# Gate and up products of 20 of 22 FFN tiles per layer: one level of Strassen's seven block products in the place of eight

## The reference

```
r = r + rms_norm(y, g_mix_post[i])
h = rms_norm(r, g_ffn_pre[i])
y = (silu(h @ w_gate[i]) * (h @ w_up[i])) @ w_down[i]      # D_FF = 2816
r = r + rms_norm(y, g_ffn_post[i])
# ... then a gated per-layer input embedding
```

## Time and profile before

| | |
|---|---|
| median of 3 runs | 3164.13 us (3160.27 to 3171.47) |
| profiled execution, span from first to last instruction | 3166.1 us |
| mean granted TensorE clock | 0.975 |
| TensorE busy | 3004.7 us, 95% |
| DVE busy | 2039.4 us, 64% |
| ACT busy | 982.9 us, 31% |
| POOL busy | 1426.3 us, 45% |
| FFN of layer 0, loop over tiles | about 759 to 1418 us of the span |
| FFN of layer 1, loop over tiles | about 2285 to 2944 us of the span |

### The profile page before, as it was taken

How to read it: one execution, slowest core, us unless ns; L and a number is a source line. 1 busy time by engine, 2 the same in 40 slices (tenths; PEclk the granted TensorE clock), 3 DMA queues, 4 the chain that set the end, 5 groups by cost and what they waited for, 6 DMA issues and landing times.

```text
span 3166.1 us, 54358 instructions
## 1 busy us (share of the span) xinstructions
PE 3004.7 (95%) x18978; PEld 2901.6 (92%) x18978; DVE 2039.4 (64%) x3685; ACT 982.9 (31%) x2197; POOL 1426.3 (45%) x933
## 2 busy tenths in 40 slices
PE   7999999999999999998988999999899999999887
PEld 7889999988999999998887988889899999999887
DVE  4657888465655655567574589965655655665675
ACT  4234777341000000004442177743300000000252
POOL 4233555554433433345554455545533433343564
PEclk9999999999999999999989999999899999999988
DMA  3497444311111111111102566522111111111111
GB/s 112 166 325 243 132 127 126 108 34 41 48 45 46 40 52 40 46 48 60 41 21 103 191 152 154 136 74 74 40 41 46 46 46 42 44 53 40 55 47 55
DMA packets 163131, 264.63 MB, mean 84 GB/s; under 512 B 95056, under 2 KB 108896, under 8 KB 162640
## 3 DMA queue, kind: packets, MB, share of 16 engines
q1 hardware_dynamic: 163024, 263.21, 26.7%
HBM read 197.74 MB, written 65.42 MB: 83 GB/s over the span
## 4 chain that ended last, share of the span: by engine, by line
PE 65%; issue 13%; POOL 11%; DVE 6%; ACT 2%; DMA 1%; POOLq 0%; SPq 0%; DVEq 0%; ACTq 0%
PE ps L1329 31%; PE ps L1039 11%; PE ps L1040 11%; PE ps L1041 11%; POOL probs L936 8%; DVE sublayer_out L2063 1%; PE ps L1060 1%; POOL pre_sums L896 1%; PE ps L1074 1%; DVE act_lo L2078 1%; POOL weight_hi L860 1%; DVE post_sums L2039 1%; DVE pre_sums L2039 1%; DVE stage_lo L2162 1%; DMA kA_lo<-stage_lo 1%
## 5 line engine op out<-in xcount | busy, mean ns | idle before, releaser
L860 POOL TENSOR_TENSOR weight_hi<-weight_raw,ones 128x1024 fp32r<-128x1024 f32 x179 | 353.0, 1972 | 1170.7 <-PE ps L1041 611.3
L2308 DVE TENSOR_TENSOR sublayer_out<-ps,sublayer_out 128x352 f32<-128x352 f32 x1008 | 527.7, 524 | 515.4 <-PE ps L1041 506.7
L1329 PE MATMUL ps<-act_hi,weight_hi 128*128 128x352 f32 x2112 | 686.4, 325 | 10.1 <-ACT ffn_act L1740 4.8
L1329 PE MATMUL ps<-act_hi,weight_lo 128*128 128x352 f32 x2112 | 683.8, 324 | 0.0
L1329 PE MATMUL ps<-act_lo,weight_hi 128*128 128x352 f32 x2112 | 683.8, 324 | 0.0
L1039 PE MATMUL ps<-act_hi,weight_hi 128*128 128x352 f32 (+2 forms) x1392 | 472.5, 339 | 32.3 <-DVE weight_lo L2107 10.8
L874 POOL TENSOR_TENSOR weight_lo<-weight_raw,weight_hi 128x1024 fp32r<-128x1024 f32 x193 | 477.3, 2473 | 54.4 <-ACT weight_hi L1730 28.3
L1040 PE MATMUL ps<-act_lo,weight_hi 128*128 128x352 f32 (+2 forms) x1392 | 459.6, 330 | 0.0
L1041 PE MATMUL ps<-act_hi,weight_lo 128*128 128x352 f32 (+2 forms) x1392 | 459.3, 330 | 0.0
L936 POOL TENSOR_TENSOR probs<-probs,row_inv 128x1024 f32<-128x1024 f32 (+8 forms) x288 | 312.1, 1093 | 291.7 <-DVE row_inv L2240 291.4
L1329 PEld LDWEIGHTS ps<-act_hi,weight_hi 128*128 128x128 f32 x2112 | 399.3, 189 | 14.0 <-issue 6.9
(11 more groups left out here) (177 smaller groups left out, 5747.2 us busy)
## 6 DMA issues: line engine op xcount, KB each, us to landing
weight_raw<-units SPq DMA_DIRECT2D x201, 512.0 KB, 3.3
k_hi<-kB_hi SPq DMA_DIRECT2D x32, 328.0 KB
qA_hi<-stage_hi SPq DMA_DIRECT2D x16, 528.0 KB, 3.7
qA_lo<-stage_lo SPq DMA_DIRECT2D x16, 528.0 KB, 4.6
q_hi<-qA_hi SPq DMA_DIRECT2D x16, 528.0 KB
q_lo<-qA_lo SPq DMA_DIRECT2D x16, 528.0 KB
kA_hi<-stage_hi SPq DMA_DIRECT2D x8, 656.0 KB, 3.0
kA_lo<-stage_lo SPq DMA_DIRECT2D x8, 656.0 KB, 4.7
```

Source lines behind the costliest of these rows:

```text
L860: pool.tensor_tensor(wh[:, slot, :], wraw[:, slot, :], ones[:, 0:1].to_broadcast((P, UW)), ALU.mult).then_inc(w_hi[slot], 1)
L1329: mm = nc.tensor.matmul(ps[:, 3 * slot + b, 0:TB], a, x, start=(k == 0 and pas == 0), stop=(k == KD - 1 and pas == 2))
L2308: V.tensor_tensor(y[:, m, c], src, y[:, m, c], ALU.add).then_inc(f_acc, 1)
```

## The change

For tiles 2 to 21 (SEVEN0 = 2) the gate and up products of token blocks 0 and 1 are computed together as one 2 x 2 block product: gate and up unit each halved over the 1024 input features (K1, K2), the tokens' blocks 0 and 1. Seven half products of 12 matmuls stand in the place of eight; token block 2 keeps its four half products, so 11 halves, 132 matmuls, in the place of 144. For it

- the weights are used as 8 half blocks of 512 columns: GATE_K1, GATE_K2, UP_K1, UP_K2, and four sums and differences (WEIGHT_SUM1 to 4), which POOL makes for each tile; ACT makes the highs of all, POOL the lows; ACT also makes the down unit's high, POOL its low;
- four sums of token rows (3 x 4 tiles in `mix`, which lies over the residual, and 4 in the place of `nh`/`nl` rows of block 1) are made once a layer, during tile 1: ACT scales the rows, POOL adds, ACT makes highs, DVE lows;
- the residual is written to DRAM before that, and read back during the last tile;
- ACT keeps one product, DVE makes five additions a tile (`seven_part`) to build the results in PSUM, and TensorE waits for two of them;
- the positions of downs, gates, muls and los move.

The core of the diff; the semaphores' arithmetic is left out.

```diff
-D_AT = [16 + (9 * d) // 2 for d in range(24)]
+D_AT = [14 + (9 * d) // 2 for d in range(24)]
-E_AT2 = [104 + 5 * d for d in range(KD)]
-LAST_ORDER = [(0, 0), (0, 1), (1, 0), (1, 1), (0, 2), (1, 2)]
+E_AT2 = [104 + (7 * d) // 2 for d in range(KD)]
+GATES = (0, 2, 1)
...
# SP
+                tile_units(0)
+                for b in range(NB):
+                    sp.wait_ge(r_done, R_AT[NORM_AT[f"s{2 + 3 * layer}", "post", b] + 1])
+                    sp.dma_start(io["residual_kept"][b], res[:, :, cols_of(b)]).then_inc(r_kept, 16)
...
+                sp.wait_ge(*product_done(layer, NF - 1, 3))
+                for b in range(NB):
+                    sp.dma_start(res[:, :, cols_of(b)], io["residual_kept"][b]).then_inc(r_back, 16)
                 for j in range(2):
                     lin_load(f"pe{layer}", j)
...
# POOL
-                    split(0, f + (u[0] + 1), (fg_rd, f * 3 + (3 * f0 + 3)))
-                    split(2, f + u[2], down_free)
-                    split(1, f + (u[1] + 1), (fu_rd, f * 3 + (3 * f0 + 3)))
+                def next_blocks(f, first=False):
+                    weight_sum(f + 1, 1, first)
+                    block_low(f + 1, WEIGHT_SUM1)
+                    weight_sum(f + 1, 2)
+                    block_low(f + 1, WEIGHT_SUM2)
+                    weight_sum(f + 1, 3, first)
+                    low(2, f + u[2])
+                    block_low(f + 1, WEIGHT_SUM3)
+                    weight_sum(f + 1, 4)
+                    block_low(f + 1, GATE_K1)
+                def tile(f):
+                    block_low(f, GATE_K2)
+                    block_low(f, WEIGHT_SUM4)
+                    block_low(f, UP_K2)
+                    block_low(f, UP_K1)
+                    next_blocks(f)
+                token_sums()
+                weight_sum(SEVEN0, 1, True)
+                block_low(SEVEN0, WEIGHT_SUM1)
+                weight_sum(SEVEN0, 2)
+                block_low(SEVEN0, WEIGHT_SUM2)
+                weight_sum(SEVEN0, 3, True)
+                for i in range(KH):
+                    token_sum4(i)
+                low(2, u[2] + 1)
+                block_low(SEVEN0, WEIGHT_SUM3)
...
# TensorE, in seven(f, among, last): (block, bank), 12 matmuls each; among() places the downs
+                    half(WEIGHT_SUM1, 1, sums_of(1), True, True, z_pr)
+                    half(WEIGHT_SUM2, 4, sums_of(2), True, True, z_pr)
+                    half(WEIGHT_SUM3, 3, sums_of(3), True, True, z_pr)
+                    half(GATE_K1, 0, rows(0, 0), True, True, z_pr)
+                    if not last:
+                        gate2_k1()
+                    pe.wait_ge(*part_added(layer, f, 1))
+                    half(GATE_K2, 0, rows(KH, 0), False, True, fg_rd, True)
+                    if not last:
+                        gate2_k2()
+                    pe.wait_ge(*part_added(layer, f, 3))
+                    half(WEIGHT_SUM4, 1, rows(KH, 1), False, True, fg_rd, True)
+                    half(UP_K2, 3, rows(0, 1), False, True, fu_rd, True)
...
+                    up2_k2()
+                    half(UP_K1, 5, rows(0, 2), False, True, fu_rd)
...
# ACT
+                def seven_tile(f, par):
+                    block_high(f, GATE_K2)
+                    block_high(f, WEIGHT_SUM4)
+                    keep_product(f)
+                    block_high(f, UP_K2)
+                    block_high(f, UP_K1)
+                    silu_in(f, 0, 0)
+                    block_high(f + 1, WEIGHT_SUM1)
+                    silu_in(f, 2, 1)
+                    block_high(f + 1, WEIGHT_SUM2)
+                    silu_in(f, 1, 2)
+                    f_high(f, par, 0)
+                    down_high(f)
+                    f_high(f, par, 1)
+                    block_high(f + 1, WEIGHT_SUM3)
+                    block_high(f + 1, GATE_K1)
+                    f_high(f, par, 2)
+                row_scales()
+                silu(1, 0)
+                sums_high(0)
+                silu(1, 1)
+                sums_high(1)
+                silu(1, 2)
+                sums_high(2)
+                sums_high(3)
+                block_high(SEVEN0, WEIGHT_SUM1, True)
+                block_high(SEVEN0, WEIGHT_SUM2, True)
+                f_high(1, 1, 0, True)
+                for i in range(KH):
+                    sum4_high(i)
+                f_high(1, 1, 1, True)
+                down_high(1)
...
# DVE
+                def seven_events():
+                    return sorted([(p, "down", d) for d, p in enumerate(D_AT)]
+                                  + [(49, "part", 1), (53, "part", 2), (58, "part", 3), (73, "gate", 0), (85, "gate", 2),
+                                     (97, "part", 4), (98, "gate", 1), (109, "part", 5), (110, "mul", 0), (115, "mul", 1),
+                                     (126, "lo", 0), (129, "lo", 1), (133, "mul", 2), (137, "lo", 2)])
...
+                events += [(50 + 6 * k, "sum", k) for k in range(12)] + [(133 + i, "sum4", i) for i in range(KH)]
```

More of the change, by code:

```diff
@@ L984, in tail_pool @@
+                low(2, u[2] + 1)
+                block_low(SEVEN0, WEIGHT_SUM3)
+                weight_sum(SEVEN0, 4)
+                block_low(SEVEN0, GATE_K1)
+                with pool.Fori(SEVEN0, NF - 1) as f:
+                    tile(f)
+                f = NF - 1
+                block_low(f, GATE_K2)
+                block_low(f, WEIGHT_SUM4)
+                block_low(f, UP_K2)
+                low(2, u[2] + f)
+                block_low(f, UP_K1)
                 adds((f"s{s + 1}", "post", 0))
@@ L1374, in among @@
                             down(f - 1, 1 - par, D_AT.index(n))
[L1376 to L1379, removed]
+                    seven(f, among)
                 def last_tile():
@@ L1388, in among @@
                             down(f, par, E_AT2.index(n), True)
[L1390 to L1392 removed]
+                    seven(f, among, True)
                     key = f"s{3 + 3 * layer}"
@@ new lines, in block_high @@
+                def block_high(f, j, first=False):
+                    F3 = f * 3 + 3 * f0
+                    if j in (WEIGHT_SUM1, WEIGHT_SUM2, WEIGHT_SUM3, WEIGHT_SUM4):
+                        n = (WEIGHT_SUM1, WEIGHT_SUM2, WEIGHT_SUM3, WEIGHT_SUM4).index(j)
+                        act.wait_ge(*sum_made(layer, f, n + 1))
+                    else:
+                        slot = int(j in (UP_K1, UP_K2))
+                        act.wait_ge(w_raw[slot], f * 16 + (u_ffn[slot] * 16 + 16))
+                    if j < 4:
+                        rd, back = ((fg_rd, 1), (fg_rd, 0), (fu_rd, 1), (fu_rd, 0))[j]
+                        act.wait_ge(rd, F3 if first else F3 - back)
+                    else:
+                        act.wait_ge(*product_done(layer, f, {GATE_K2: 1, WEIGHT_SUM4: 2, UP_K2: 3, UP_K1: 5}[j]))
+                    sem_, _ = block_hi_done(layer, f, j)
+                    nc.scalar.activation(weight_block(wh, j), block_source(j), ACT.Copy).then_inc(sem_, 1)
@@ L2347, in tile, with seven_tile @@
                             ple_low(x)
+                        elif what == "sum":
+                            sum_low(x)
+                        elif what == "sum4":
+                            sum4_low(x)
                         else:
                             lo(f, par, x)
+                def seven_tile(f, par, events, order=GATES):
+                    for _, what, x in events:
+                        if what == "down":
+                            down(f - 1, x)
+                        elif what == "early":
+                            down(f, x, last=True)
+                        elif what == "part":
+                            seven_part(f, x)
+                        elif what == "gate":
+                            seven_gate(f, x, order)
+                        elif what == "mul":
+                            seven_mul(f, x, order)
+                        elif what == "ple_low":
+                            ple_low(x)
+                        else:
+                            lo(f, par, x)
+                def seven_events():
[3 more added lines that the diff above has]
+                                     (126, "lo", 0), (129, "lo", 1), (133, "mul", 2), (137, "lo", 2)])
                 pre = [(s, "pre", b) for b in range(NB)]
@@ L2786 @@
     dram("p_parts", (2, NB, P, 2, 2, TB))
+    dram("residual_kept", (NB, P, KD, TB))
     for part in ("hi", "lo"):
```

255 lines of the change are left out of this document (236 added, 19 removed).

## The result

The changed kernel takes 3240.15 us (median of 4 runs, 3239.51 to 3244.96); the kernel before, on the same chip, 3164.76. The ratio is 1.024, 95% interval 1.0226 to 1.0255: slower by 2.4%. The forecast of 3211 us had the sign and 46 of the 75 us; the time lies 5 us above the range's top of 3235. Medians and ratios here are those of undisturbed runs; one of the eight runs with mul 2 between took 7224 us and is left out.

A forecast was written before the change was run, and what follows sets the result against it. TensorE, busy 95% of the span, was taken to bound the kernel. 3166.1 - 76.9 + 86.2 + 38 = 3213.4 us of span; the profiled execution lies 2.0 above the median, so 3211 us, own range 3185 to 3232, whole range 3117 to 3235.

The forecast's parts named there:

- What is taken away: Loop over tiles: 12 TensorE matmuls less in each of 20 tiles of 2 layers, 480 x 0.1603 = 76.9 us saved.
- Work inside the tile at no cost: Inside a tile: POOL's, ACT's and DVE's moved or new work fills none of them and is priced at nothing.
- The boundary: Tile's end: held lo's delay down 0's addition, so TensorE stops 2.2 us a tile; with the last tile, +86.2 us.
- the 3.5: Last tile of each layer: down 2 stands at product 15, so TensorE's stop there is 3.5 us.
- The start: Tiles 1 and 2: sums queue on POOL and DVE ahead of the down unit; +19 us a layer, +38 in all.
- the clock, above. 3%: Rival: each boundary stop followed by 24 slots at lower clock, up to 3.8 us in 38 tiles, up to 3357 us; 3%.
- the stop of 1.96 us: Trace row at 1446.6: clock stayed at 1.00 behind this TensorE stop; taken as speaking against the lower-clock rival.
- the likely one: Said of the lower-clock rival at tile boundaries: by the Trainium skill's section it would be likely; given 3%, up to 3357 us.
- the los fit: Rival at the tile's end: los fit between POOL's instructions, DVE's tail is through by E+4.65; 3110 or 3125 us; 24%.
- lo 0 wins its race: Rival at the tile's end: lo 0 goes ahead of POOL's low; stop 1.2 us a tile, 3173 us; 14%.

The follow-up runs named there:

- mul 2 between: Changed kernel with mul 2 moved from behind lo 1 to in front of it in DVE's order, nothing else: 3174.51 us, ratio 1.0033 to the kernel before.

## Why the prediction was right or wrong

- **What is taken away**, 76.9 us: right within 5. The tile without a stop has a period of 32.84, not 32.70; over 36 tiles 5 us less gain. What makes the 0.14 is not shown.
- **Work inside the tile at no cost**: right. Half instructions on POOL take 1.28 to 1.30 us (1.29 worked out) and 1.58 when a lo is held (+0.29); the loop has no stop at a weight block, and without the stop at down 2 nothing else is late there.
- **The boundary**, 2.2 us a tile: right in mechanism, order and size. The stop is 1.87 and the loss 34.97 - 32.84 = 2.13. The restart costs 0.26 where the sum had 0.10. In the last tile the 3.5 came together by luck: the stop on down 0's addition is 2.3, and 0.8 on one of the five additions (a part) and 0.46 on the down unit stand beside it, which the prediction doesn't name.
- **The start**, 19 us a layer: right in size (tile 2's down 2 comes at 780.39, where the kernel before, 1.2 us behind at 722, had it at 763.1 in the pace of the earlier trace rows, +17.3), and its parts were the ones named: a stop of 5.23 on the sum lows, 5.42 on the down unit, 1.00 on down 0. Not in its make-up: two stretches of 6.8 us at half clock, up to 2.5 us each, are in the 17.3.
- **The clock**: here the prediction failed. The span without falls in the loops is 3238.7 - 16 x 1.53 = 3214.2 us, and the sum said 3213.4 (the terms above miss by 5 one way and by 6 the other, so that this agrees within 1 us is partly luck). The failed step is the rival "the clock, above. 3%". It was weighed by one row, the stop of 1.96 us behind which the clock stayed at 1.00. That row was no evidence to rest 38 tiles on: in the changed kernel the clock stays at 1.00 behind 10 of 18 equal stops, too. And the rival was priced as all or nothing, 3.8 us in each of 38 tiles and 3357 us, with nothing between; what came is 1.53 in 16 of 36. A part-way case would have lifted forecast or top by 25.
- The Trainium skill, "TensorE: Matmul & The Clock Gate", section "HAM oscillation — how this bites in real kernels", which the prediction set against its row, says that a loop that waits in every pass can lose the clock in every pass. The runs agree in kind, in 8 and in 14 passes of 18 for stops of 1.87 or 2.5 us; for 0.65 and 1.4 us it happens in none. The case that the Trainium skill describes there waits for some 3 to 5 us in each pass, longer than any stop of these loops, so "the likely one" was more than it says for a stop of 2 us.
- **The rivals** that the los fit (24%) and that lo 0 wins its race (14%) didn't come. lo 0 starts 0.14 behind POOL's low at 914, and was worked out at 0.27 behind.

## What to carry to other kernels

Where a bound engine waits in every pass, look at what stands behind a slow instruction in the other engine's list, and not at the slow instruction: the same held subtractions cost 77 us (36 x 2.13) with down 2 at product 23 and nothing with it at 38, or in another order. When a stop of 1 to 3 us is forecast for a loop, make a case of its own for a clock that falls behind some of the stops; one quiet stop elsewhere in the trace does not rule it out, and half a microsecond less of a stop can be worth more than the stop. A change that removes work from the bound engine brings all its other work closer to that engine's schedule, and should come with the list of the next engine worked out just as closely.

## What was not expected of the hardware

- Behind stops of equal length the clock falls at some and not at others (8 of 18 at 1.87 us, in the same pattern in both layers), and at none of 36 at 1.4 us: a change of 0.5 us in one wait moves the time by 41 us, of which the waits themselves are 17.
- A DVE subtraction with two SBUF inputs takes up to 2.7 us beside GpSimd (2.72 in the earlier trace rows, 2.65 for lo 0 in the loop with mul 2 between; 0.52 alone); with one input in PSUM 0.52 beside the same GpSimd instruction, which then loses only 0.03 in the place of 0.29.
- TensorE loses 0.25 us more than the stop that the profile shows, at every stop length tried.
